# Two transformer blocks on one core: expert blocks nested, the modulation's rest between projections, a shorter list of waits before near attention

## What is computed

```
# first block
mod = silu(c) @ w_ada + b_ada                      # six vectors of 1024: shift1 scale1 gate1 shift2 scale2 gate2
h = modulate(rmsnorm(x), shift1, scale1)
proj = h @ w_in                                    # retention q k v g, delta q k v z, two small gates
x = x + gate1 * (concat(retention(...), gated_delta_rule(...)) @ w_out)
h2 = modulate(rmsnorm(x), shift2, scale2)
x = rmsnorm(x + gate2 * hierarchical_moe(h2))      # top-1 group of 4, then top-2 of its 8 experts
# second block
x = x + concat(neighbourhood_attention(...), bidirectional_gla(...)) @ w_out_2
x = rmsnorm(x + square(relu(rmsnorm(x) @ w_ff1)) @ w_ff2)
```

## Time and profile before

| what | value |
|---|---|
| median of 3 runs (lowest to highest) | 3558.24 us (3552.54 to 3558.36) |
| the profiled execution | 3554.09 us, its span 3551.7 us |
| PE busy / DVE / ACT / POOL | 93% / 27% / 18% / 14% of the span |
| front, to its `meet` | 0 to 299.4 us |
| retention | 299.4 to 427.0 us |
| experts, of which 35 blocks are used | 1071 to 1882.9 us |
| mix, first product of its projections at | 1907.4 us |
| near attention | 2395.1 to about 2542 us |

### The profile page before, as it was taken

One profiled execution on the slowest core, in us unless ns is written; L12 is line 12 of the kernel. 1 busy time (PEld: TensorE's weight loads), 2 busy tenths in 40 slices (PEclk: granted clock), 3 DMA queues, 4 the chain that ended last, 5 costly groups with the idle time before them and its releaser, 6 DMA issues.

```text
span 3551.7 us, 30482 instructions
## 1 busy us (share of the span) xinstructions
PE 3290.5 (93%) x11998; PEld 1915.5 (54%) x11998; DVE 957.0 (27%) x1816; ACT 622.4 (18%) x1405; POOL 504.6 (14%) x543
## 2 busy tenths in 40 slices
PE   4997899788968999999995999989999999999999
PEld 2444544687426777777772445547644444444444
DVE  4214435565131111111113314549510100000101
ACT  3001132222111111111112221117520000000000
POOL 2003332453202000000002100016400000000000
PEclk9998999899978999999997999999999999999999
DMA  5435832000219998888865110011211111232222
GB/s 217 131 94 64 229 32 51 1 25 32 100 38 369 382 341 334 335 334 334 335 236 194 59 48 1 24 47 46 72 48 36 40 38 36 64 108 77 95 77 77
DMA packets 248555, 461.71 MB, mean 130 GB/s; under 512 B 27953, under 2 KB 110289, under 8 KB 244945
## 3 DMA queue, kind: packets, MB, share of 16 engines
q1 hardware_dynamic: 224433, 398.39, 33.5%
q0 software_dynamic: 9360, 34.08, 2.6%
q10 hardware_dynamic: 14608, 27.14, 2.0%
HBM read 481.33 MB, written 61.97 MB: 153 GB/s over the span
## 4 chain that ended last, share of the span: by engine, by line
PE 45%; issue 21%; POOL 2%; DVE 2%; DMA 1%; ACT 0%; POOLq 0%; SPq 0%; ACTq 0%; DVEq 0%
PE bank L2817 12%; PE bank L2848 12%; PE bank L2112 5%; PE bank L2690 3%; PE bank L2284 3%; PE bank L2282 2%; PE bank L2615 2%; PE bank L2623 2%; PE bank L229 1%; POOL e_rows L1706 1%; PE bank L2497 0%; PE bank L2494 0%; PE bank L1459 0%; PE bank L2506 0%; DMA n_bias<-bias_rows 0%
## 5 line engine op out<-in xcount | busy, mean ns | idle before, releaser
L1767 PE MATMUL bank<-e_w,e_xsT 128*128 128x256 f32 x2240 | 491.3, 380 | 1.6 <-DVE e_xsT L1807 1.6
L1767 PEld LDWEIGHTS bank<-e_w,e_xsT 128*128 128x128 f32 x2240 | 427.0, 191 | 74.8 <-issue 18.2
L2848 PE MATMUL bank<-w_ff,uT 128*128 128x512 f32 x1024 | 441.8, 594 | 3.6 <-DVE hT L2905 3.6
L2817 PE MATMUL bank<-hT,w_ff 128*128 128x512 f32 x1024 | 439.8, 592 | 0.0
L2848 PEld LDWEIGHTS bank<-w_ff,uT 128*128 128x128 f32 x1024 | 195.0, 191 | 250.2 <-issue 243.9
L2817 PEld LDWEIGHTS bank<-hT,w_ff 128*128 128x128 f32 x1024 | 194.4, 190 | 243.9 <-issue 243.9
L1786 PE MATMUL bank<-e_w,e_hidT 128*128 128x512 f32 x560 | 246.1, 592 | 0.0
L473 PE MATMUL bank<-w_in,hT 128*128 128x512 f32 x512 | 223.4, 597 | 4.1 <-DVE hT L385 2.3
L2112 PE MATMUL bank<-w_gla,nT 128*128 128x512 f32 x384 | 168.2, 598 | 1.3 <-ACT nT L2076 1.3
L758 PE MATMUL bank<-hT,w_qkv 128*128 128x512 f32 x384 | 167.0, 593 | 0.0
L1786 PEld LDWEIGHTS bank<-e_w,e_hidT 128*128 128x128 f32 x560 | 103.7, 190 | 117.2 <-issue 117.2
(11 more groups left out here) (450 smaller groups left out, 3830.2 us busy)
## 6 DMA issues: line engine op xcount, KB each, us to landing
e_w<-in_w SPq DMA_DIRECT2D x144, 2048.0 KB
w_ff<-in_w_ff SPq DMA_DIRECT2D x96, 512.0 KB, 3.6
wa<-in_w_ada SPq DMA_DIRECT2D x24, 1024.0 KB, 6.3
y_rows<-e_y ACTq DMA_DIRECT2D x35, 512.0 KB, 6.9
y_rows<-zero SPq DMA_DIRECT2D x1, 16384.0 KB, 112.4
w_in<-in_w_in SPq DMA_DIRECT2D x4, 2048.0 KB, 15.9
w_qkv<-in_w_in SPq DMA_DIRECT2D x12, 512.0 KB, 6.9
w_gla<-in_w_in SPq DMA_DIRECT2D x3, 2048.0 KB, 14.3
```

Source lines behind the costliest of these rows:

```text
L1767: t = pe.matmul(experts_up_bank(k, part, j), b.xsT[n][:, f, :], w[:, f, part * HALF:(part + 1) * HALF], start=f == 0, stop=f == NK - 1)
L2817: t = pe.matmul(k.bank[2 * (j % 2) + h][:, :], w[:, f, :], hT[:, f, h * BANK:(h + 1) * BANK], start=f == 0, stop=f == NK - 1)
L2848: t = pe.matmul(k.bank[2 * n + h][:, :], b.uT[:, f, m * P:(m + 1) * P], b.ring[j % SLOTS][:, h * BANK:(h + 1) * BANK], start=f == 0, stop= ...
```

## The change

Four places are changed; buffers are moved in SBUF to make room, which changes no instruction.

1. The ada steps are brought forward, so that all 24 are done with the third column chunk. In the fourth chunk PE does the one-column products and three of the products by ones behind tile 1, and the fourth behind tile 4; DVE copies them out behind tiles 3 and 5. SP's order of `w_ada` and `w_in` loads is changed to match. `w_z` is loaded ahead of the `meet`, as soon as the last ada step has freed the ring.
2. `experts_blocks` is nested: each unsure block's question stands inside the block before it, so that the first unused block jumps past all that are left, to one `skip`.
3. `meet` after the experts leaves SP out; the two loads of `w_gla` are issued by ACT at the start of its part of `mix`.
4. `n_bias` is loaded ahead of `n_val_odd`, SP no longer waits for them, DVE waits for the bias at the start of near attention, and PE for `n_val_odd` before each product that reads it.

```diff
-    def meet(self):
+    def meet(self, sync=True):
...
-        for engine in (nc.tensor, nc.vector, nc.scalar, nc.gpsimd, nc.sync):
+        engines = (nc.tensor, nc.vector, nc.scalar, nc.gpsimd) + ((nc.sync,) if sync else ())
+        for engine in engines:
             m = self.barrier.up()
             engine.drain().then_inc(*m.inc)
-        for engine in (nc.tensor, nc.vector, nc.scalar, nc.gpsimd, nc.sync):
+        for engine in engines:
             engine.wait_ge(*m)
...
     front_sync(k, s, b)
+    retention_prefetch(k, s, ret_s, wz)
...
-    for at in range(2, 4):
-        for q in range(NK + RING + 4 * (at - 2), NK + RING + 4 * (at - 1)):
+    for at, parts in ((2, range(11, 14)), (3, range(14, 20))):
+        for q in parts:
             front_ada_load(k, s, b, q)
         sy.wait_ge(*s.projected((at - 1) * NT))
         front_w_load(k, s, b, at)
-    for q in range(NK + RING + 8, 3 * NK):
+    for q in range(20, 3 * NK):
         front_ada_load(k, s, b, q)
...
-            if m % 2:
-                front_ada_vector(k, s, b, NK + 4 * at + m // 2)
-    v.wait_ge(*s.rest_made(1))
...
+            for _ in range(front_ada_steps(at, m)):
+                front_ada_vector(k, s, b, q)
+                q += 1
+            if at == 3 and m == 3:
+                v.wait_ge(*s.rest_made(1))
...
+            if at == 3 and m == 5:
+                v.wait_ge(*s.rest_made(5))
+                for n, dst in enumerate((b.gate1[0][:, :], b.gate1[1][:, :], gate2[:, 0:BANK], gate2[:, BANK:])):
+                    v.tensor_copy(dst, k.bank[(5, 6, 7, 4)[n]][:, :]).then_inc(*V.up().inc)
+
+
+def front_ada_steps(at, m):
+
+    if m % 2 == 0 or at == 3:
+        return 0
+    return 2 if at and m % 4 == 3 else 1
...
-    pe.wait_ge(*s.ada_step(3 * NK))
-    front_columns(k, b, k.bank[4], (3, 4)).then_inc(*s.rest_made.up().inc)
...
+            if at == 3 and m in (1, 4):
+                front_rest(k, s, b, m // 4)
+
+
+def front_rest(k, s, b, n):
+
+    pe = k.nc.tensor
+    if n == 0:
+        pe.wait_ge(*s.ada_step(3 * NK))
+        front_columns(k, b, k.bank[4], (3, 4)).then_inc(*s.rest_made.up().inc)
+    else:
+        pe.wait_ge(*s.rest_out(1))
+    for at, bank in (((2 * D, 5), (2 * D + BANK, 6), (5 * D, 7)), ((5 * D + BANK, 4),))[n]:
+        pe.matmul(k.bank[bank][:, :], k.c("ones"), b.acc[:, at:at + BANK], start=True, stop=True).then_inc(*s.rest_made.up().inc)
...
+def retention_prefetch(k, front_s, s, wz):
+
+    k.nc.sync.wait_ge(*front_s.ada_step(3 * NK))
+    k.nc.sync.dma_start(wz[:, :, :], k.io["w_in"][:, 7 * BANK:8 * BANK].rearrange("(k p) c -> p k c", p=P)).then_inc(*s.wz_loaded.up().inc)
...
     sy = k.nc.sync
-    sy.dma_start(wz[:, :, :], k.io["w_in"][:, 7 * BANK:8 * BANK].rearrange("(k p) c -> p k c", p=P)).then_inc(*s.wz_loaded.up().inc)
     sy.dma_start(rpb_rows, wide(k.io["rpb"], 2, W)).then_inc(*s.rpb_spread.up().inc)
...
-        k.meet()
-        k.retire(s)
+        k.meet(sync=False)
+        return s
...
-SURE, GROUP = 2 * T // P, 4
-
-
-def experts_blocks(engine, used, work, skip):
-
-    for at in range(SURE):
+SURE = 2 * T // P
+
+
+def experts_blocks(engine, used, work, skip, at=0):
+
+    if at < SURE:
         work(at)
-    for first in range(SURE, BLOCKS, GROUP):
-        with engine.If(used > first):
-            work(first)
-            for at in range(first + 1, first + GROUP):
-                with engine.If(used > at):
-                    work(at)
-                with engine.Else():
-                    skip(at, 1)
+        experts_blocks(engine, used, work, skip, at + 1)
+    elif at < BLOCKS:
+        with engine.If(used > at):
+            work(at)
+            experts_blocks(engine, used, work, skip, at + 1)
         with engine.Else():
-            skip(first, GROUP)
+            skip(at, BLOCKS - at)
...
-            a.sem_inc(stored[(at + n) % 2].sem, 16 * ((blocks + 1) // 2))
+            a.sem_inc(stored[(at + n) % 2].sem, 16 * ((blocks + 1 - n) // 2))
...
-    for j in (1, 2):
-        mix_load(k, s, b, j)
...
 def mix_scalar(k, s, b):
 
+    for j in (1, 2):
+        mix_load(k, k.nc.scalar, s, b, j)
     mix_scalar_rows(k, s, b, 0)
...
     sy.wait_ge(*d.unit_out(NT))
+    sy.dma_start(near.bias[:, :, :], bias_rows).then_inc(*d.bias_got.up().inc)
     for lo, n, src in ((0, NT, near.val_even[W:P, 0:NT, :]), (W, NT - 1, near.val_even[0:W, 1:NT, :])):
         sy.dma_start(near.val_odd[lo:lo + W, 0:n, :], src).then_inc(*d.val_odd_got.up().inc)
-    sy.dma_start(near.bias[:, :, :], bias_rows).then_inc(*d.bias_got.up().inc)
-    sy.wait_ge(*d.bias_got(1))
-    sy.wait_ge(*d.val_odd_got(2))
...
+    k.nc.vector.wait_ge(*d.bias_got(1))
     s = k.on("q_ready scored neg_max exp_ready sum_inverse weights_ready rows_turned pT_out av_made mix_out")
...
         pe.wait_ge(*s.pT_out(u + 1))
+        if lo % 2:
+            pe.wait_ge(*d.val_odd_got(2))
```

More of the change, by code:

```diff
@@ L358, in front_vector @@
         front_turned_vector(k, s, hT, affine, i)
+    q = NK
     for at in range(4):
@@ L476, in front_tensor @@
                 front_turn(k, s, b, m + 2)
-    pe.wait_ge(*s.ada_step(3 * NK))
-    front_columns(k, b, k.bank[4], (3, 4)).then_inc(*s.rest_made.up().inc)
-    for j, part in enumerate((2, 5)):
-        for h in range(2):
-            at = part * D + h * BANK
-            if j and h:
-                pe.wait_ge(*s.rows_out_a(4 * NT // 2))
-            pe.matmul(k.bank[(5, 6, 7, 0)[2 * j + h]][:, :], k.c("ones"), b.acc[:, at:at + BANK], start=True, stop=True).then_inc(*s.rest_made.up().inc)
+            if at == 3 and m in (1, 4):
[9 more added lines that the diff above has]
+        pe.matmul(k.bank[bank][:, :], k.c("ones"), b.acc[:, at:at + BANK], start=True, stop=True).then_inc(*s.rest_made.up().inc)
 def rotary_vector(k, s, b):
@@ L2231, in gla @@
     k.meet()
-    k.retire(s[0] + s[1] + d)
+    k.retire(s[0] + s[1])
+    return d
 def near_areas(k):
@@ L2531, in neighbourhood @@
     interleave(*(near_gpsimd(k, s, b, n) for n in range(NSETS)))
-    interleave(*(near_tensor(k, s, b, n) for n in range(NSETS)))
+    interleave(*(near_tensor(k, s, d, b, n) for n in range(NSETS)))
     k.meet()
-    k.retire(s)
+    k.retire(s + d)
 def near_rows(n):
@@ L2952, in build @@
         b, conv_b = front_areas(k), delta_conv_areas(k)
-        z, retT, deltaT = k.at("z", front_at(106), P, NT, BANK), k.at("retT", front_at(138), P, RH, T), k.at("deltaT", front_at(122), P, RH, T)
+        z, retT, deltaT = k.at("z", front_at(106), P, NT, BANK), k.at("retT", front_at(140), P, RH, T), k.at("deltaT", front_at(124), P, RH, T)
         dtok, d, res_b = k.at("dtok", front_at(0), P, NT, 3 * BANK), delta_gates(k), residual_areas(k, b.gate1)
-        front(k, b, hT, affine, cols, gate2)
+        ret_s, wz = retention_signals(k), k.at("w_z", front_at(124), P, NK, BANK)
+        front(k, b, hT, affine, cols, gate2, ret_s, wz)
         conv_s = delta_conv_signals(k)
-        retention(k, b, hT, retT, z, y_rows, rpb_rows, conv_s, conv_b)
+        retention(k, ret_s, b, hT, retT, z, wz, y_rows, rpb_rows, conv_s, conv_b)
         delta_conv(k, conv_s, conv_b, hT, dtok, z, d, rpb_rows, bias_rows)
@@ L2966, in build @@
             ahead = itertools.chain(mix_prefetch(k, mix_s, mix_b, x_rows[0]), decay_prefetch(k, decay_s, decay_b))
-            experts_pass(k, affine[:, 2, :], affine[:, 3, :], tokens, experts, xn_rows, y_rows, ahead, lambda: mix_indices(k, mix_s, mix_b))
+            experts_s = experts_pass(k, affine[:, 2, :], affine[:, 3, :], tokens, experts, xn_rows, y_rows, ahead, lambda: mix_indices(k, mix_s, mix_b))
         near = near_areas(k)
@@ L2970, in build @@
         decay(k, decay_s, decay_b, mix_s, mix_b.nT)
-        gla(k, mix_s, mix_b, decay_s, decay_b, bias_rows, near)
-        k.retire(mix_s + decay_s)
+        near_s = gla(k, mix_s, mix_b, decay_s, decay_b, bias_rows, near)
+        k.retire(mix_s + decay_s + experts_s)
         out_s, out_b = out_signals(k), out_areas(k, near, mix_b.qkvr, cols)
@@ L2975, in build @@
         out_prefetch(k, out_s, out_b)
-        neighbourhood(k, near)
+        neighbourhood(k, near_s, near)
         out_sync(k, out_s, out_b, mlp_s, mlp_b, x_rows[1], x_rows[2])
```

49 lines of the change are left out of this document (23 added, 26 removed).

## The result

The changed kernel took 3524.38 us (median of 4 runs, 3522.59 to 3529.37) against 3557.02 for the kernel before on the same chip: ratio 0.991, 95% interval 0.9897 to 0.9922. The forecast was 3532 us (3522 to 3543), and a gain: both hold. The profiled execution took 3522.59 us with a span of 3520.5, 31.2 us shorter than that of before. The forecast said 23.8. Most of the extra comes from one stage, the experts' end, which came out against the forecast.

The account below looks back on a forecast made before the run. PE was busy 93% of the span, so only holes between stages could be gained: -15.3 + 0.7 - 9.2 = -23.8 us. From the profiled 3554.09 that gives 3530.3; half of 4.15 on top makes 3532, range 3522 to 3543.

Parts of the forecast that it names:

- experts' end: From PE's last expert product to the stage's end: 0.7 us later, bounds 2.5 earlier to 2.5 later.
- The modulation's rest: Front: one-column products and products by ones move between projections, so retention starts at 293.7, 5.7 us earlier.
- The charge of 2.3 us for the clock: Front: loss from a low granted clock after the first one-column products, 2.3 us, between nothing and twice that.
- `w_z` and the rotary: Retention: with `w_z` early, PE waits for POOL's rotary instead; with the front's 5.7, next stage 15.3 us earlier, at 411.7.
- The 2.3 us charged for the clock: Retention: slow clock on work behind PE's wait for the rotary, 2.3 us, between nothing and 3.
- The fill: Retention: fill of `y_rows` lands by 407.6, 4 us margin; as rival it holds the stage's end, 3542, chance 0.10.
- All five now go from about 1866.3 on: Experts: POOL's five remaining loads wait out a far jump of about 5 us, the last issued at 1871.3, not 1870.55.
- Near attention: Near attention's start: without SP's waits 9.7 us earlier, less 0.5 us waiting for the bias, so -9.2 us.
- The 0.5 us charged for the bias: Near attention's start: DVE's wait for the bias to land, 0.5 us, between nothing and 5.6.
- The rival, a shared flight: Near attention: three transfers go side by side, DVE waits 5.6 us for the bias; sum -18.7, 3537, chance 0.12.
- Questions not taken: Experts: untaken branches cost nothing; the rival had 5 us at each of 19 unsure blocks, 95 us, 3627, chance 0.02.
- the third rival: Experts: short jump or quicker landing of POOL's loads, stage gives 4 us instead of taking 0.7; -28.5, 3527, chance 0.13.

Follow-up runs that it names:

- part 1 alone: Kernel before plus only the front's change (early ada steps, products between projections, `w_z` loaded ahead of the `meet`): 3541.41 us, ratio 0.9962.
- the repeat: The changed kernel measured once more, unchanged, against the kernel before: 3526.34 us, ratio 0.9905.
- the variant with `w_z` ahead: Changed kernel with four more `w_z` steps at retention's start, the last variant tried: stage 3.1 to 3.4 us shorter, 3526.34 us, ratio 0.9909 to before.

## Why the prediction was right, and where not

- **The modulation's rest**, forecast retention's start at 293.7: measured 293.01 in the first profile, 292.40 with part 1 alone, 294.59 in the repeat, and 294.6 to 297.0 in five variants with the same front. The kernels with the front of before spread as well, from 299.27 to 303.26, and the first one-column products tell why: they take 3.9 us in some executions, 6.99 in others and 4.4 to 4.9 in three (last section). Like against like, the front gains 6.3 to 7.0 us with 3.9 and 4.7 to 6.4 with 6.99, around the 5.7 forecast. The charge of 2.3 us for the clock was 0 in the first profile and about 1.7 in seven others. Where it was 0, some 1.7 us went in the second chunk: there is a wait for `w_in` of 1.96 us ahead of it, 1.7 to 2.1 in the others too, but in most of them the clock stayed at 1.00 behind it, and in this profile it read 0.69.
- **`w_z` and the rotary**, forecast 15.3 us earlier at the next stage: measured 16.4. POOL ended tile 1's rotary 10.7 us after the start, exactly as carried over from the earlier trace rows. The 2.3 us charged for the clock were about 1.7: from 302 to 306 it read 0.50, and the transposes behind the rotary and the four `w_z` records behind them took that much longer than the same work at full clock. The fill had 12 us of margin where I had counted 4: it was issued at 294.11, not 295.2, and landed in 104.7 us, not 112.4.
- **Experts' end**, forecast +0.7: measured -5.2. The failed step is "All five now go from about 1866.3 on", that is, the five microseconds of the far jump kept as exposed. I read the earlier trace rows as two kinds of jump with two prices. The runs say that the place comes first: behind 7.03 us of queued products the far jump lets POOL go as soon as the near one (0.78 and 0.77 us), and a drain put there makes it 4.77. Behind a drain the kind may count as well: the near jumps took 0.2 to 2.7 us there, those past four and past eight blocks 4.37 and 4.36. The rule that I cited speaks of the fetch alone: by the Trainium skill, "Runtime: NRT & Kernel Launch", section "Instruction fetch mechanics", a taken branch out of the loaded window must fetch its target. That agrees with the 4.37 us behind a drain. The trace doesn't say that the stall is this fetch; what decides here is whether anyone waits for it. The change leaves one such jump, and it is the hidden one. The forecast had listed as a sign of being wrong an experts' barrier more than 2 us earlier against PE's last product, and that is what came. The rest of that step held: POOL stayed last, by 0.6 us where SP was put back into the barrier, and leaving SP out was worth nothing.
- **Near attention**, forecast -9.2: measured -8.7. The 0.5 us charged for the bias was 0; ACT's last copy came 0.9 us later, counted from the first gather of `y`. The rival, a shared flight, was a real danger: it costs 7.3 us when the order of issue is turned. By the Trainium skill, "DMA: Bandwidth & Descriptors", "HWDGE ordering", each DMA engine takes the descriptors of one queue in the order of issue; the flights of 8.5 us ahead of the values, and 15.49 and 16.0 behind them, agree.
- **Questions not taken** cost nothing, as said. From the load of rows that POOL issues during the last sure block to the one during the last used block, 19 unsure blocks later, it is 417.85 to 417.86 us in all fourteen profiles, nested or not (1435.70 to 1853.55 before, 1418.36 to 1836.22 after). The row "between" of the first table can't show that: it runs from 1430.3 to 1437.0 us over the profiles.
- **Sum**: -23.8 forecast, -31.2 by the spans. The experts' 5.9 us are most of the difference, the rest is a us each from the front with retention and from stages that the change doesn't touch, less 0.5 from near attention. That the time still fell into the range is owed to the third rival, which let the experts' end give 4 us and put the whole at 3527 with a chance of 0.13: it is nearer to what came (3524.38, and 3526.34 in the repeat) than the forecast's 3532. Three stages were right by their mechanism, the experts' end wasn't.

## What to carry to other kernels

Before pricing a jump, ask what is queued on its engine: here the branch past unused blocks is free right behind 7 us of products and costs 4 to 5 us behind a drain, so arrange that only one is taken and that it comes first. When several transfers are issued together, put the one that is read first at their head; here that was worth 7.3 us, in a part that gained 8.7. Bring the work forward that a chain waits for (here the ada steps); moving the chain itself added little. And where a load was hidden badly at a stage's start, look what becomes last once it is early (here the rotary), since the hole it leaves can take work from the end.

## What was not expected of the hardware

The same code doesn't run at the same pace from one execution to the next, and the granted clock tells only part of why. The front's first one-column products, in the first profile of the changed kernel and in that of the variant with `w_z` ahead (timelines of PE):

```profile
47.79 3.88 PE L463 MATMUL bank<-consts,mod_acc 128*128 128x1 f32 x32 [0.19 <-DVE mod_acc L340]
```
```profile
48.28 6.99 PE L462 MATMUL bank<-consts,mod_acc 128*128 128x1 f32 x32 [0.15 <-DVE mod_acc L339]
```

Both begin with the clock at 1.00, that is 2.4 GHz, and in the second it reads 1.00 throughout. The first is followed by some five us at 0.50, 1.2 GHz, the second by none, but at the start of the second chunk the second is still 4.0 us behind (122.39 against 118.43), 0.5 of which it was late before. Why the second is slow stays open; seven of the fourteen profiles show 6.99 us, with old and new fronts alike, and the other seven 3.9 to 4.9. In the delta stage, where nothing was changed, the repeat lost 5.4 us against the first profile of the same kernel. One window of both, from the same product to the same product (busy times of PE, PEld, DVE, ACT and POOL, granted clock, DMA share, GB/s), the first profile and then the repeat:

```profile
618.24:867.82 249.58, 211.45 (x1712) 201.29 (x1712) 147.29 (x248) 70.43 (x121) 116.82 (x103) 0.94 0.05 18
```
```profile
618.63:873.58 254.95, 217.19 (x1712) 206.82 (x1712) 147.37 (x248) 70.62 (x121) 117.03 (x103) 0.91 0.05 18
```

PE works off the same 1712 records in both, in 211.45 us with the clock at 0.94 and in 217.19 at 0.91. Together the two places are worth up to 9 us, where executions of one kernel differ by up to 12, and they cover gains like the 3 us of the last variant. And the five unused loads of POOL decide the experts' end throughout: the last one takes 6.5 to 8.3 us to land, which is 1 to 2 us of spread that no edit here explains, and then 4.06 us follow on POOL's queue, the same in every profile in which POOL comes last.
